# Weight sums of the Winograd down projection moved from VectorE to GpSimd, low parts made from PSUM copies

## What is computed

```python
h = rmsnorm(x, p['norm_ffn_pre'][i])
f = jnp.square(jax.nn.relu(h @ p['w_up'][i])) @ p['w_down'][i]
x = x + rmsnorm(f, p['norm_ffn_post'][i])
```

## Time and profile before

| what | us |
|---|---|
| median of 3 executions | 1777.16 (1773.88 to 1780.49) |
| the profiled execution, its own time | 1778.79 |
| its span in the trace | 1777.0 |
| TensorE busy | 1686.0 (95%) |
| VectorE busy | 1154.2 (65%) |
| ScalarE busy | 835.8 (47%) |
| GpSimd busy | 579.6 (33%) |
| granted TensorE clock, mean | 0.99 |

### The profile page before, as it was taken

One profiled execution on the slowest core, in us unless ns is written; L12 is line 12 of the kernel. 1 busy time (PEld: TensorE's weight loads), 2 busy tenths in 40 slices (PEclk: granted clock), 3 DMA queues, 4 the chain that ended last, 5 costly groups with the idle time before them and its releaser, 6 DMA issues. The chain is left out here.

```text
span 1777.0 us, 31700 instructions
## 1 busy us (share of the span) xinstructions
PE 1686.0 (95%) x12611; PEld 1611.1 (91%) x12611; DVE 1154.2 (65%) x2100; ACT 835.8 (47%) x1606; POOL 579.6 (33%) x361
## 2 busy tenths in 40 slices
PE   6999999999999999999999999999999999999996
PEld 5987877998999999998899999987998899999996
DVE  6437777315774838477879797967306774838477
ACT  6326666324433434345555666565424534434342
POOL 1231211231443343432125344440341452343431
PEclk9999999999999999999999999999999999999998
DMA  6621111121222322231223223331221222313221
GB/s 227 209 77 55 55 66 31 60 84 48 96 95 72 107 67 101 72 101 54 75 77 105 98 91 94 100 104 61 72 83 40 104 84 83 108 60 108 72 96 54
DMA packets 51491, 153.11 MB, mean 86 GB/s; under 512 B 12400, under 2 KB 14160, under 8 KB 51088
## 3 DMA queue, kind: packets, MB, share of 16 engines
q1 hardware_dynamic: 43968, 139.99, 23.2%
q10 hardware_dynamic: 7376, 11.10, 2.0%
HBM read 144.16 MB, written 6.47 MB: 85 GB/s over the span
## 5 line engine op out<-in xcount | busy, mean ns | idle before, releaser
L1189 PE MATMUL ps<-big_hi,w_hi 128*128 128x288 f32 x2528 | 560.0, 302 | 12.6 <-DVE relu L1969 6.3
L1189 PE MATMUL ps<-big_lo,w_hi 128*128 128x288 f32 x2528 | 541.6, 298 | 7.2 <-DVE big_lo L1666 7.1
L1189 PE MATMUL ps<-big_hi,w_lo 128*128 128x288 f32 x2528 | 545.3, 295 | 0.0
L2412 POOL TENSOR_TENSOR w_lo<-raw,w_hi 128x1024 fp32r<-128x1024 f32 x116 | 284.2, 2451 | 680.2 <-ACT w_hi L611 569.9
L1189 PEld LDWEIGHTS ps<-big_hi,w_hi 128*128 128x128 f32 x2528 | 410.0, 190 | 21.0 <-issue 18.3
L1189 PEld LDWEIGHTS ps<-big_lo,w_hi 128*128 128x128 f32 x2528 | 403.0, 189 | 12.5 <-DVE big_lo L1666 11.6
L1189 PEld LDWEIGHTS ps<-big_hi,w_lo 128*128 128x128 f32 x2528 | 408.4, 189 | 0.1
L1481 PE MATMUL ps<-col_hi,w_hi 128*128 128x288 f32 x896 | 267.5, 299 | 16.9 <-DVE mix L2059 15.8
L1481 PE MATMUL ps<-col_hi,e_lo 128*128 128x288 f32 x896 | 264.4, 295 | 0.0
L1481 PE MATMUL ps<-col_lo,w_hi 128*128 128x288 f32 x896 | 264.0, 295 | 0.0
L611 ACT ACTIVATE w_hi<-raw 128x1024 fp32r<-128x1024 f32 x176 | 185.6, 1055 | 151.3 <-DMA raw<-in_slabs 86.2
(11 more groups left out here) (223 smaller groups left out, 2283.8 us busy)
## 6 DMA issues: line engine op xcount, KB each, us to landing
raw<-in_slabs SPq DMA_DIRECT2D x238, 512.0 KB, 3.3
row<-acs_prompt ACTq DMA_DIRECT2D x16, 384.0 KB, 3.8
bias<-in_alibi SPq DMA_DIRECT2D x12, 256.0 KB, 2.6
x<-in_x SPq DMA_DIRECT2D x2, 1152.0 KB, 8.3
out_h<-state ACTq DMA_DIRECT2D x4, 384.0 KB, 2.6
out_y<-x SPq DMA_DIRECT2D x2, 576.0 KB, 2.8
raw<-in_slabs SPq DMA_DIRECT2D x4, 256.0 KB, 3.7
kms<-in_mk SPq DMA_DIRECT2D x2, 512.0 KB, 5.1
```

The lines of the kernel that those rows point to most:

```text
L1189: ins = pe.matmul(ps[:, bank + h, 0:hi_c - lo_c], weight(w, s, kt), a[:, k0 + kt, lo_c:hi_c], start=start, stop=stop, skip_group_check=True)
L2412: pool.tensor_tensor(w_lo[:, s % RING], raw[:, s % RING], w_hi[:, hi_place(s)].bitcast(F32), ALU.subtract).then_inc(lo_done, 1)
```

## The change

- GpSimd makes the weight sums (`weight_sum` moves from the VectorE program to the GpSimd program, word for word but for the engine). Its order in a pair is entry k = 0, 1, 2, 4, 5, 3, 6: low part of A11, the four sums, low parts of A12 and A22. For p = 1 it first waits until all activation low parts of the chunk are done.
- ScalarE copies the high part of each sum, once made, into a PSUM bank (`sum_copy`, banks 6 and 7 in turn); a copy waits for the low part that used its bank before.
- VectorE makes the low parts of the sums as `e_raw` minus the PSUM copy, spread over the pair in which they are used.
- ScalarE's order: the high part of A22 of a pair (k = 6) is made before those of k = 4 and 5; that of pair 0 ahead of the last hidden square of the up projection; a slab's high part in each layer's first chunk one step earlier; after a layer the square of the last tile's second half comes after the first `big_hi` of the next projection.
- TensorE waits for all four low parts of the last pair before its bank 6 is written by the norm's sum.

```diff
@@ ScalarE
+                def sum_copy(c, p, k):
+                    place, nth = fifo_place(layer, c, ENTRIES * p + k), 4 * pair_number(layer, c, p) + sums_before(c, p, k)
+                    act.wait_ge(*hi_of_entry(layer, c, p, k))
+                    if nth > 1:
+                        act.wait_ge(s_lo_done, nth - 1)
+                    act.activation(s_copy(layer, c, p, k), e_hi[:, place].bitcast(F32), ACT.Copy).then_inc(s_copied, 1)
...
                 def down(c):
-                    entry_hi(c, ENTRIES - 1)
                     for p in range(PAIRS_DOWN):
-                        for k in range(ENTRIES):
+                        fourth = ENTRIES - 1 if is_last(c, p) else ENTRIES - 2
+                        turned = p + 1 < PAIRS_DOWN and is_last(c, p + 1)
+                        for i in range(ENTRIES):
+                            k = i if turned or p + 1 == PAIRS_DOWN else (0, 1, 2, 3, 6, 4, 5)[i]
                             if p + 1 < PAIRS_DOWN:
                                 entry_hi(c, ENTRIES * (p + 1) + k)
+                                if products(c, p + 1)[k] in (("S", 1), ("S", 2), ("S", 3)):
+                                    sum_copy(c, p + 1, k)
...
+                            if i == 0:
+                                sum_copy(c, p, fourth)
...
@@ VectorE, down
+                        if p:
+                            weight_lo(c, p, 2)
                         if p == 0:
                             columns_second(c, 3)
                         end(0)
                         dve.wait_ge(freed, g0 + 2 * p)
                         add_to(mix_half[:, c11], ps[:, a, 0:HALF]).then_inc(read_done, 1)
+                        if p:
+                            weight_lo(c, p, 3)
...
+                        weight_lo(c, p, 4)
                         if c == FF_CHUNKS - 1 and p:
                             post_add(2 * p - 2)
                             post_add(2 * p - 1)
                         end(4)
                         dve.wait_ge(read_done, reads + 2)
                         add_to(mix_half[:, c11:c11 + 4:3], ps[:, b:b + 2, 0:HALF]).then_inc(read_done, 1)
...
@@ GpSimd
+                        if p == 1:
+                            pool.wait_ge(col_lo_done, 4 * PAIRS_DOWN * (FF_CHUNKS * layer + c + 1))
+                        for k in (0, 1, 2, 3, 5, 6, 4) if is_last(c, p) else (0, 1, 2, 4, 5, 3, 6):
+                            entry_lo(c, p, k)
```

More of the change, by code:

```diff
@@ L652, in last_square @@
             def last_square():
+                if n.t:
+                    act.wait_ge(freed, n.g - 1)
+                    act.activation(sq[:, 1, span(1)], mix[:, KT - 1, span(1)], ACT.Square).then_inc(sq_ready, 1)
                 act.wait_ge(freed, n.g)
@@ L920, in up @@
                         hidden_square(c, m)
+                        if first and m == 0:
+                            split_to(n.s + RING)
                         columns_hi(c, m)
@@ L1515, in last_pair @@
                     column_product(c, p, 4, other, False).then_inc(half_done, 1)
+                    pe.wait_ge(s_lo_done, 4 * pair_number(layer, c, p) + 4)
                     column_product(c, p, 5, f, True, lambda: half_sum(0)).then_inc(product_done, 1)
@@ L2053, in weight_lo @@
                     dve.wait_ge(s_summed, 4 * pair_number(layer, c, p) + read_by)
-                    dve.tensor_tensor(e_lo[:, place], e_raw[:, place], e_hi[:, place].bitcast(F32),
+                    dve.tensor_tensor(e_lo[:, place], e_raw[:, place], s_copy(layer, c, p, k),
                                       ALU.subtract).then_inc(s_lo_done, 1)
@@ L2441, in ffn, with place_of, weight_sum @@
             def ffn(layer):
+                def place_of(c, p, s):
+                    k = products(c, p).index(("S", s))
+                    return k, fifo_place(layer, c, ENTRIES * p + k)
+                def weight_sum(c, p, s):
+                    number, first = pair_number(layer, c, p), pair_slab(layer, c, p)
+                    k, place = place_of(c, p, s)
+                    a11, a12, a21, a22 = [a_block(layer, c, p, ("A", i, j)) for i in range(2) for j in range(2)]
+                    for t in (first, first + 1):
+                        pool.wait_ge(raw_in[t % RING], 16 * (t // RING + 1))
+                    pool.wait_ge(*place_free(layer, c, ENTRIES * p + k))
+                    if sums_before(c, p, k):
+                        pool.wait_ge(s_summed, 4 * number + sums_before(c, p, k))
+                    part = lambda i: e_raw[:, place_of(c, p, i)[1]]
+                    if s == 3:
+                        ins = pool.tensor_tensor(part(3), a11, a21, ALU.subtract)
+                    elif s == 4:
+                        ins = pool.tensor_tensor(part(4), a12, part(2), ALU.subtract)
+                    elif is_last(c, p):
+                        if s == 2:
+                            ins = pool.tensor_tensor(part(2), a22, part(3), ALU.subtract)
+                        else:
+                            ins = pool.tensor_tensor(part(1), part(2), a11, ALU.add)
+                    elif s == 1:
+                        ins = pool.tensor_tensor(part(1), a21, a22, ALU.add)
+                    else:
+                        ins = pool.tensor_tensor(part(2), part(1), a11, ALU.subtract)
+                    ins.then_inc(s_summed, 1)
                 def entry_lo(c, p, k):
                     kind, place = products(c, p)[k], fifo_place(layer, c, ENTRIES * p + k)
+                    if kind[0] == "S":
+                        weight_sum(c, p, kind[1])
+                        return
                     pool.wait_ge(*hi_of_entry(layer, c, p, k))
```

105 lines of the change are left out of this document (27 added, 78 removed).

## The result

The changed kernel takes 1769.1 us (median of 9 runs, 1767.4 to 1773.8) where the kernel before takes 1779.1 beside it (9 runs): a ratio of 0.9949, 95% interval 0.9937 to 0.9962. The medians are 10.0 us apart, about half of the 19.1 that were forecast; by the ratio the gain is 0.51%, or 9 us. The profiled execution of the changed kernel took 1767.9 us, its span is 1766.1.

What follows compares the result with a forecast made beforehand. TensorE was taken as nearly always busy, so only its stops, mainly for VectorE's late adds, could be won. Won 25.2 + 1.0 + 1.1 = 27.3, lost 8.2, net 19.1: 1777.2 becomes 1758 us, range 1749 to 1769.

Steps and rivals of the forecast that it cites:

- stops of before, all gone or replaced: Down projection: 28 stops of TensorE for VectorE's add to `mix`, 23.5 us idle, priced at 25.2 with restarts.
- pair 2, last chunks: Last chunk of each layer: squares wait for pair 3's third sum, 0.2 us lost in place of 0.77.
- Part 1: Down projection, pairs 1 to 3: adds on time, GpSimd keeps up, pair 1's stops go, 1.59 + 0.44 in eight chunks.
- Part 2: Pair 0 of each chunk: the 0.69 stop before product 4 becomes about 0.5 before product 2, bounds 0 and 1.2.
- another 0.7 if GpSimd's sums delay the last eviction: Pair 0: possible 0.7 us beyond the upper bound of 1.2 for the new stop before product 2.
- Part 3: Last chunk of each layer: late squares delay the add, 1.9 us lost before product 6 of pair 1, twice.
- part 4: Reordered steps outside the down projection: `big_hi` sooner, 1.0 us, and less wait in first chunks, 1.1 us.
- A: Rival, down projection: no new stop, all 27.3 us won, 1750; chance 0.15.
- C: Rival, down projection: GpSimd becomes the bound, gain used up from 1.78 us a step, 1797 at 1.9; chance 0.05.
- D: Rival, down projection: the change does not free VectorE, pair 1's stops stay, 16.2 us, 1774; chance 0.09.
- B: Rival, down projection: GpSimd stays slow at 1.5 us a step, 17.2 lost, 10 won, 1767; chance 0.19.

Runs made afterwards that it cites:

- run 10: Changed kernel with pair 0's third low part behind the last eviction and GpSimd's A22 low part held until the activation low parts are done: ratio 0.9932.
- run 1: Changed kernel with ScalarE, in a layer's last chunk, squaring the two finished rows before it makes the next pair's first sum high: ratio 0.9914.
- run 3: Changed kernel with GpSimd's first sum in each layer's first chunk held until VectorE made the activation low parts of tiles 4 and 5: ratio 0.9968.
- run 6: Changed kernel with last-chunk squares early, pair 0's third low part behind the last eviction, GpSimd's `split_lo` after layer 0 held for the square sums: ratio 0.9903.
- 2: Changed kernel with VectorE, in pair 0 of each chunk, making the add after product 0 before the activation sum `columns_second`: ratio 0.9938.
- 5: Changed kernel with VectorE's low part of pair 0's third sum moved behind the last eviction of the up phase: ratio 0.9956.

## Why the prediction was wrong

The time fell outside the range by a hair, and short of the forecast by half. Step by step, in us:

| term | forecast | measured |
|---|---|---|
| stops of before, all gone or replaced | +25.2 | +25.2 |
| steps outside: `big_hi` and relu | +2.1 | +2.6 (0.95 + 2 x 0.83) |
| pair 0, six later chunks | -3.0 | -3.2 (6 x 0.53) |
| pair 0, two first chunks | -1.0 | -5.0 (1.42 + 2.39 + 1.19) |
| product 6 of pair 1, last chunks | -3.8 | -4.8 (2 x 2.39) |
| pair 2, last chunks | -0.4 | 0 |
| last pair of layer 0 | 0 | -1.2 |
| one stretch of half clock more | 0 | -1.7 |
| net | 19.1 | 11.9 |

The FFNs became 11.0 shorter, the medians are 10.0 apart. Of the 0.9 between 11.9 and 11.0, 0.4 is a wait for `big_lo` behind layer 0, which grew from 0.80 to 1.22.

*Part 1* was right: pair 1's stops went, and GpSimd keeps up. But it has less than the 1.3 us to spare that run 10 took from it; by my sum it had more.

*Part 2* was right in the later chunks to 0.03 us, cause included (run 10). **It failed in the first chunks**: it put one stop of 0.5 in each of the eight chunks, 1.0 us for the two first ones, and these cost 5.0 in this trace. The trace of before already showed that they differ. They alone stop before product 2 of pair 0:

```profile
489.32 0.19 PEld L1481 LDWEIGHTS ps<-col_hi,w_hi 128*128 128x128 f32 x1 [0.69 <-DVE mix L2059]
...
1418.06 0.19 PEld L1481 LDWEIGHTS ps<-col_hi,w_hi 128*128 128x128 f32 x1 [0.71 <-DVE mix L2059]
```

In a first chunk TensorE has just waited for the norm, and VectorE is already behind. GpSimd's sums, moved ahead into the up phase, fall on its columns: 3.80 us for three low parts instead of 1.80, and 4.75 to 4.92 in some traces. The same collision is in the later chunks (3.98), where VectorE otherwise waits 2.6 us for TensorE before an eviction, and it costs nothing. The stop before product 2 follows from how late VectorE starts the last eviction. Counted from the down projection's first weight load, and without a stop in between, it starts at 0.81, 1.47, 1.54, 1.71, 2.65 and 2.84, and the stops are 0.47, 1.13, 1.20, 1.36, 2.33 and 2.32 (a later chunk, then first chunks of the changed kernel's two traces and of run 1).

Two things stay open. The size is not fixed: the second trace of the changed kernel has 1.36 and 1.20, 2.7 us in all, and run 1, whose first chunks are the same code, 2.32 twice, 4.8. And no run shows how much of it the collision makes: run 3 took it away and held the sums so long that the last eviction was as late (2.65 and 2.83), and the stop as long. I had written "another 0.7 if GpSimd's sums delay the last eviction"; it was 1.7 to 4.0 us in the two layers. Where TensorE happens to run at half clock after relu's stop, VectorE catches up and the 1.36 inside product 0 goes.

*Part 3* had the mechanism, and its size 1.9 was short by 0.5. A GpSimd sum that waits for the one before it starts 0.17 later, so the sums come every 1.46, not 1.30, and the square sum took 0.94 beside GpSimd.

*The clock* was not in the sum. Before has three stretches of 1.7, each behind a stop outside the down projection; the change brings them down (3.33 twice to 2.50, 1.99 to 1.04) but puts up three of 2.33, where the longest wait for the add was 1.6 and none had such a tail. This is also why part 4 is worth more than its idle time.

*The last pair of layer 0* I hadn't looked at: VectorE makes its square sums there just when GpSimd's `w_lo` begin (3.85 us for the two), and with these held (run 6) the stop is gone.

*Of the rivals*, A is excluded by the stops of 0.47, C by the absence of waits for GpSimd, D by pair 1. B's time, 1767, is nearest, and its 1.46 for a step is real for the sums; but its bill (4.2 in each last chunk, pair 0 at 0.9) isn't what the trace shows, so that its time fits is luck.

## What to carry to other kernels

A stop is not priced by its idle time alone: look at the granted clock behind the stops of the kernel before, and count a new long stop with its tail, here 2.3 + 1.7 us about four times in five. The move was won only with the copies: without them the time was that of before (1.0003). When work is moved from one engine to another, look for its new neighbours in each phase apart, first and last chunk above all, and not in the steady one; the collision counts where the engine has no slack. And a stop has more than one support: three of the fixes (2, 5, 10) took away exactly what the trace named and found another almost as large (0.43, 0.47, 0.34 for 0.47).

## What the runs showed of the hardware

- In the FFNs, where TensorE's work is dense, the granted clock often fell to 0.50 for 3.4 us at the end of a stop of 1.99 us and more (59 of 74), from 3.1 us before TensorE was back to 1.5 after, and cost 1.7 us where TensorE worked all through. After stops of 0.9 to 1.72 it never did (63). Outside the FFNs 19 of 68 such stretches had no stop of 1.9 or more at hand.
- A VectorE instruction with both inputs in SBUF that meets a GpSimd step ends some 0.6 us after that step (a sum of 0.76 took 0.98 and 1.45 and ended 0.60 and 0.62 behind it), three in a row 3.80 to 4.92 instead of 1.80; with one input in PSUM all 128 took 0.67 to 0.69. GpSimd loses less, 1.60 instead of 1.30.
- A GpSimd sum that waits for the one before it starts 0.17 us after that one's end.
- A ScalarE copy of 128 x 512 from SBUF into PSUM takes 0.60 us, a high part of the same size into SBUF 0.62.
